# Weight sums of eight seven-product chunks: accumulating DMAs issued by GpSimd instead of VectorE additions

## The reference, cut to what matters

```
(sq, sk, sv, dq, dk, dv, iq, ik, iw, hq, hf, hi, hg,
 g_sb, g_dsa, g_hg) = jnp.split(h @ w_in_l, _split_points(), axis=-1)
...
mixed = jax.nn.sigmoid(g_sb) * y_sb + jax.nn.sigmoid(g_dsa) * y_dsa + jax.nn.sigmoid(g_hg) * y_hg
return mixed @ w_out_l
```

## Time and profile before

| what | value |
|---|---|
| median of three runs | 1595.08 us |
| span of the profiled execution | 1592.4 us |
| what lies around the span (median less span) | 2.7 us |
| PE (TensorE matmul) busy in the span | 1458.7 us (92%) |
| DVE (VectorE) busy | 740.9 us (47%) |
| ACT (ScalarE) busy | 314.6 us (20%) |
| POOL (GpSimd) busy | 22.7 us (1%) |
| moved by DMA | 380.17 MB, mean 239 GB/s |

### The profile page before, as it was taken

One profiled execution on the slowest core, in us unless ns is written; L12 is line 12 of the kernel. 1 busy time (PEld: TensorE's weight loads), 2 busy tenths in 40 slices (PEclk: granted clock), 3 DMA queues, 4 the chain that ended last, 5 costly groups with the idle time before them and its releaser, 6 DMA issues.

```text
span 1592.4 us, 19689 instructions
## 1 busy us (share of the span) xinstructions
PE 1458.7 (92%) x8156; PEld 1004.4 (63%) x8156; DVE 740.9 (47%) x1465; ACT 314.6 (20%) x655; POOL 22.7 (1%) x41
## 2 busy tenths in 40 slices
PE   8999999999999999999999999999999576577578
PEld 5687889999545788898999446755554133133132
DVE  3646576766666646567666656544331000001001
ACT  2234431122001125430222001334410000000000
POOL 0000000000000000000000002100000000000000
PEclk9999999999999999999999999999999788788689
DMA  9547224454453633334444446655799999999998
GB/s 319 191 159 245 90 100 153 157 199 169 158 175 108 213 127 138 107 107 159 159 169 182 179 158 204 226 185 186 287 392 426 427 426 426 428 427 426 428 419 318
DMA packets 114921, 380.17 MB, mean 239 GB/s; under 512 B 10836, under 2 KB 23252, under 8 KB 104144
## 3 DMA queue, kind: packets, MB, share of 16 engines
q1 hardware_dynamic: 111952, 369.53, 60.6%
q0 software_dynamic: 2880, 9.36, 1.9%
HBM read 377.25 MB, written 5.73 MB: 241 GB/s over the span
## 4 chain that ended last, share of the span: by engine, by line
PE 79%; DMA 17%; DVE 2%; SPq 1%; ACT 1%; issue 1%; DVEq 0%; ACTq 0%
DMA ring<-in_w 17%; PE bank L1508 13%; PE bank L1561 12%; PE bank L1144 11%; PE bank L1151 8%; PE bank L1324 5%; PE bank L1712 4%; PE bank L1298 3%; PE bank L1250 3%; PE bank L1274 2%; PE bank L1610 2%; PE bank L1738 1%; PE bank L1481 1%; PE bank L1483 1%; PE bank L1200 1%; PE bank L1226 1%
## 5 line engine op out<-in xcount | busy, mean ns | idle before, releaser
L1144 PE MATMUL bank<-hT,ring 128*128 128x256 f32 x832 | 185.4, 381 | 0.0
L1144 PEld LDWEIGHTS bank<-hT,ring 128*128 128x128 f32 x832 | 156.0, 190 | 21.9 <-issue 1.0
L1712 PE MATMUL bank<-ring,region 128*32 128x512 f32 x208 | 116.4, 724 | 48.8 <-DMA region<-in_w 48.8
L1712 PE MATMUL bank<-region 128*32 128x512 f32 x512 | 116.6, 722 | 48.5 <-DMA ring<-in_w 48.5
L1561 PE MATMUL bank<-region 128*128 128x512 f32 x320 | 140.6, 592 | 0.0
L1561 PEld LDWEIGHTS bank<-region 128*128 128x128 f32 x320 | 60.5, 190 | 74.6 <-issue 74.6
L1508 PE MATMUL bank<-region 128*128 128x128 f32 x768 | 100.5, 275 | 0.0
L1508 PEld LDWEIGHTS bank<-region 128*128 128x128 f32 x768 | 93.0, 192 | 0.0
L1712 PEld LDWEIGHTS bank<-region 128*32 128x32 f32 x512 | 29.1, 130 | 94.0 <-issue 94.0
L1712 PEld LDWEIGHTS bank<-ring,region 128*32 128x32 f32 x208 | 25.8, 130 | 83.3 <-issue 83.3
L1151 PE MATMUL bank<-ring,hT 128*128 128x512 f32 x160 | 71.7, 596 | 0.0
(11 more groups left out here) (488 smaller groups left out, 2421.6 us busy)
## 6 DMA issues: line engine op xcount, KB each, us to landing
region<-in_w SPq DMA_DIRECT2D x43, 2048.0 KB, 38.6
ring<-in_w SPq DMA_DIRECT2D x30, 2048.0 KB, 37.7
ring<-in_w_in SPq DMA_DIRECT2D x26, 2048.0 KB, 8.2
ring<-in_w_up SPq DMA_DIRECT2D x16, 2048.0 KB, 8.3
ring<-in_w_down SPq DMA_DIRECT2D x32, 1024.0 KB, 6.3
own_slot<-in_w SPq DMA_DIRECT2D x7, 2048.0 KB, 43.3
ring<-in_w_out SPq DMA_DIRECT2D x6, 2048.0 KB, 7.9
region<-in_w SPq DMA_DIRECT2D x22, 512.0 KB, 9.3
```

The costliest lines, as they stand in the source:

```text
L1144: t = mm(b[:, 0:T], w[:, k, :], act[:, k, :], start=(k == 0), stop=(k == KD - 1))
L1712: t = mm(b[32 * e:32 * e + 32, :], xg[:, k, 32 * e:32 * e + 32], four[e][c][:, 512 * (k % 2):512 * (k % 2) + 512], start=(k == 0), stop=(k ...
```

## The change

In eight of the ten chunks (all but `iq` and `hh` of layer 0) VectorE's four sums are taken out and GpSimd issues seven DMAs of 512 KB. Three are plain loads from the weights in DRAM: s1 gets a21, s2 gets a11, s4 gets a12. Four add into their destination: s1 += a22 (from DRAM), s2 += s1, s3 += a11 (from DRAM, onto a21 in the ring slot, so after the chunk has arrived), s4 += s2. The last three additions of the chain s1, s2, s4 each wait for the one before. An addition is all that such a DMA does here, so the signs of the scheme change: s2 = s1 + a11, s3 = a11 + a21, s4 = a12 + s2, with the signs carried by the activations' sums and the reassembly. `rooms` are the events after which the places of s1 and of s2 and s4 are free.

```
+ADDED = (("hf", 0), (4, 0), (5, 0), ("iq", 1), ("hh", 1), ("hf", 1), (4, 1), (5, 1))
...
-    s += [("gt",), ("gw", 4), ("ho",)]
+    s += [("gt",), ("ho",)]
...
-    s += [("gw", 5), ("gc", 4, 0)] + att[22:] + gm(4, 1, *GATE_ORDER) + [("gc", 4, 1), ("gs",), ("gf", 4, 0), ("gf", 4, 1)]
+    s += [("gc", 4, 0)] + att[22:] + gm(4, 1, *GATE_ORDER) + [("gc", 4, 1), ("gs",), ("gf", 4, 0), ("gf", 4, 1)]
...
+            def added_sums(l, c, rooms, parts):
+                (a11, a12), (a21, a22) = dram_quarters(l, c)
+                s1, s2, s3, s4 = row_weight_sums(l, c) if c in ROW_SEVENS else gate_sums(l, c)
+                n = 16 * (ADDED.index((c, l)) + 1)
+                pool.wait_ge(*rooms[0])
+                pool.dma_start(s1, a21).then_inc(sum_begun[0], 16)
+                pool.wait_ge(*rooms[1])
+                pool.dma_start(s2, a11).then_inc(sum_begun[1], 16)
+                pool.dma_start(s4, a12).then_inc(sum_begun[2], 16)
+                pool.wait_ge(sum_begun[0], n)
+                pool.dma_start(s1, a22, accum_op=ALU.add).then_inc(sum_added[0], 16)
+                pool.wait_ge(sum_begun[1], n)
+                pool.wait_ge(sum_added[0], n)
+                pool.dma_start(s2, s1, accum_op=ALU.add).then_inc(sum_added[1], 16)
+                for part in parts:
+                    pool.wait_ge(*arrive[chunk_at[(l, part)]])
+                pool.dma_start(s3, a11, accum_op=ALU.add).then_inc(sum_added[2], 16)
+                pool.wait_ge(sum_begun[2], n)
+                pool.wait_ge(sum_added[1], n)
+                pool.dma_start(s4, s2, accum_op=ALU.add).then_inc(sum_added[3], 16)
+            def forget_sums(l):
+                added_sums(l, "hf", [bk.full((l, "ty1", "iq"))] * 2, ["hf"])
+            def late_gate_sums(l):
+                added_sums(l, 4, [bk.full((l, "gy", "hf", 1))] * 2, [("g", 4)])
+                added_sums(l, 5, [bk.full((l, "ty1", "hh")), bk.full((l, "hl", LAST, 1))], [("g", 5)])
             rows, cols = 15, 31
+            forget_sums(0)
             pool.wait_ge(seg_normed, 1)
...
             pool.wait_ge(kv_stored, 16)
+            late_gate_sums(0)
+            added_sums(1, "iq", [bk.full((0, "ty1", "wo", 0))] * 2, ["iq"])
+            added_sums(1, "hh", [bk.full((0, "ty1", "wo", 1)), bk.full((0, "down", PRODUCTS[-1]))], ["hi", "hg"])
+            forget_sums(1)
+            late_gate_sums(1)
...
-                        pe.wait_ge(quarter_sums_ready, 12 * l + 4 * SEVENS.index(c) + GATE_ORDER.index(m) - 1)
+                        pe.wait_ge(*sum_there(l, c, GATE_ORDER.index(m) - 2))
...
-                link(V.tensor_tensor(r2, b22, r1, ALU.subtract))
+                link(V.scalar_tensor_tensor(out=r2, in0=b22, scalar=-1.0, in1=r1, op0=ALU.mult, op1=ALU.subtract))
...
-                V.tensor_tensor(pairs[:, 0:2, 1, :], eight[:, :, 1, :], bc(m5.unsqueeze(1), [2, P]), ALU.add)
+                V.tensor_tensor(gate_corners[t2][:, 1, :], gate_corners[t2][:, 1, :], m5, ALU.add)
+                V.scalar_tensor_tensor(out=gate_corners[t2][:, 3, :], in0=gate_corners[t2][:, 5, :], scalar=-1.0, in1=m5,
+                                       op0=ALU.mult, op1=ALU.subtract)
```

More of the change, by code:

```diff
@@ L545, in build @@
              "sums_ready neg_rs_ready up_sums_ready h_sums_ready m1_copied last_half_loaded row_quarter_sums raw_row_sums row_m1_copied rows_copied row_corners_used wo_quarter_sums wo_row_sums wo_m1_copied wo_added p_quarter_sums p_row_sums p_m1_copied p_rows_copied "
-             "quarter_sums_ready row_sums_ready seven_m1_copied seven_sigmoids").split()]
+             "row_sums_ready seven_m1_copied seven_sigmoids").split()]
         gate_row = [sem(f"gate_row{j}") for j in range(2)]
+        sum_begun = [sem(f"sum{j}_begun") for j in (1, 2, 4)]
+        sum_added = [sem(f"sum{j}_added") for j in (1, 2, 3, 4)]
         chunks = chunks_of_layer(0) + chunks_of_layer(1) + chunks_of_block2()
@@ L848, in gate_sums, with dram_quarters, sum_there @@
             return own_[:, 3], low_quarters[:, 0], a21, low_quarters[:, 1]
+        def dram_quarters(l, c):
+            w = a["w_in"][l].rearrange("(h k p) n -> h p k n", h=2, p=P)
+            first = {"iq": COL["iq"], "hh": COL["hi"], "hf": COL["hf"]}.get(c, COL["gsb"] + 512 * c if isinstance(c, int) else 0)
+            return [[w[kh][:, :, first + 256 * fh:first + 256 * fh + 256] for kh in range(2)] for fh in range(2)]
+        def sum_there(l, c, j):
+            return sum_added[j], 16 * (ADDED.index((c, l)) + 1)
         def row_weights(l, c):
@@ L1242, in row_products @@
                         pe.wait_ge(raw_row_sums, l + 1)
-                    if 2 <= n < 6:
-                        pe.wait_ge(row_quarter_sums, 8 * l + 4 * ROW_SEVENS.index(c) + n - 1)
+                    if 2 <= n < 6 and l:
+                        pe.wait_ge(*sum_there(l, c, n - 2))
+                    elif 2 <= n < 6:
+                        pe.wait_ge(row_quarter_sums, 4 * ROW_SEVENS.index(c) + n - 1)
                     if m in ROW_STARTS:
@@ L2322, in quarter_sums_of_rows @@
                 s1, s2, s3, s4 = row_weight_sums(l, c)
-                n = 8 * l + 4 * ROW_SEVENS.index(c)
+                n = 4 * ROW_SEVENS.index(c)
                 V.tensor_tensor(s1, a21, a22, ALU.add).then_inc(row_quarter_sums, 1)
                 dve.wait_ge(row_quarter_sums, n + 1)
-                V.tensor_tensor(s2, s1, a11, ALU.subtract).then_inc(row_quarter_sums, 1)
-                V.tensor_tensor(s3, a11, a21, ALU.subtract).then_inc(row_quarter_sums, 1)
+                V.tensor_tensor(s2, s1, a11, ALU.add).then_inc(row_quarter_sums, 1)
+                V.tensor_tensor(s3, a11, a21, ALU.add).then_inc(row_quarter_sums, 1)
                 dve.wait_ge(row_quarter_sums, n + 2)
-                V.tensor_tensor(s4, a12, s2, ALU.subtract).then_inc(row_quarter_sums, 1)
+                V.tensor_tensor(s4, a12, s2, ALU.add).then_inc(row_quarter_sums, 1)
             def raw_sums(l):
@@ L2351, in row_corner_sums @@
                 m5 = psum[bk.bank((l, "ty0", c))][:, 256:512]
-                free(V.tensor_tensor(pairs[:, 0:2, 1, :], eight[:, :, 1, :], bc(m5.unsqueeze(1), [2, 256]), ALU.add),
-                     (l, "ty0", c))
-                free(V.tensor_tensor(row_corners[:, 2, :], row_corners[:, 5, :], read((l, "ty1", c))[:, 0:256], ALU.subtract),
+                V.tensor_tensor(row_corners[:, 1, :], row_corners[:, 1, :], m5, ALU.add)
+                free(V.scalar_tensor_tensor(out=row_corners[:, 3, :], in0=row_corners[:, 5, :], scalar=-1.0, in1=m5,
+                                            op0=ALU.mult, op1=ALU.subtract), (l, "ty0", c))
+                free(V.tensor_tensor(row_corners[:, 2, :], read((l, "ty1", c))[:, 0:256], row_corners[:, 5, :], ALU.subtract),
                      (l, "ty1", c))
@@ L2476, in gate_row_sums @@
                 r1, r2, r3, r4 = [gate_rows_sums[late][:, j] for j in range(4)]
-                link(V.tensor_tensor(r1, b12, b11, ALU.subtract))
-                link(V.tensor_tensor(r2, b22, r1, ALU.subtract))
+                link(V.tensor_tensor(r1, b11, b12, ALU.subtract))
+                link(V.scalar_tensor_tensor(out=r2, in0=b22, scalar=-1.0, in1=r1, op0=ALU.mult, op1=ALU.subtract))
                 V.tensor_tensor(r3, b22, b12, ALU.subtract)
-                V.tensor_tensor(r4, r2, b21, ALU.subtract).then_inc(row_sums_ready, 1)
+                V.tensor_tensor(r4, r2, b21, ALU.add).then_inc(row_sums_ready, 1)
             def gate_corner_sums(l, c, t2):
```

29 lines of the change are left out of this document (6 added, 23 removed).

## The result

The changed kernel takes 1621.17 us (median of four runs, 1619.21 to 1624.42) against 1594.98 us for the kernel before on the same chip (four runs): 26.2 us slower, a ratio of 1.0167 with a 95% interval of 1.0156 to 1.0179. The prediction was 1595.1 us with a range up to 1612. It is wrong, and its direction is that of the rival *the chain of additions ends late*, which had a chance of 0.24.

What follows compares the result with a forecast made beforehand. TensorE was taken to bound the mixers, up to about 1150 us, and the streaming of expert weights the rest. Zero from VectorE's relief plus zero from new waits left 1595.1 us, no change; range 1593.5 to 1612.

Steps and rivals of the forecast that it cites:

- the chain of additions ends late: Rival: `hf` of layer 1 and chunk 5 in both layers end late, slower from 6.7 us per addition; chance 0.24.
- VectorE's relief: VectorE ends some 34 us less busy, worth nothing on the path because TensorE waits for none of it.
- zero: Gain in the mixers from VectorE's 34 us: none, with 3.2 us of listed waits the most that could come.
- the listed waits: TensorE's waits in the two mixers, 1.8 and 1.4 us, together 3.2, which removing VectorE's sums would not shorten.
- the sum of the chain: Loads, queue and three additions: 27.6 us in 29.05 at layer 1's `hf`, 22.2 in 25.86 at chunk 5.
- my upper bound, the copy done twice: Price limit of one adding DMA: the dearer plain transfer of 512 KB twice in a row, 14.2 us.
- Room enough: DMA engines, busy 0.54 around `hh` and `hf`, can take 28 MB more, 123 us spread over 600 us.
- Its formula: Late-chain rival's waits at `hf` of layer 1 and chunk 5 twice: 8 us per addition gives 1610, 10 gives 1628.
- the other case: The forecast of no change, 1595.1 us: every chain ends before the product that reads it; chance 0.65.
- the threshold of 6.7: Average us per addition up to which no change holds; there `hf` waits 2.5 and chunk 5 twice 0.3.
- The stopped issuer: Rival: GpSimd cannot hand out transfers while VectorE runs; layer 1's `hf` is 13.6 us late, 1609; chance 0.04.
- Issuing: GpSimd's handing out of the 56 DMAs at 0.56 us each, 32 us; chunk 5's three issues 1.7 us.

Runs made afterwards that it cites:

- e6_no_sums: Changed kernel with the eight chunks' sums made by nobody and no wait of TensorE for them: 1594.02 us, ratio 1.0000 to the kernel before.
- Experiment 3: Changed kernel with the four adding DMAs of each chunk made plain copies, same order and waits: 1595.26 us, ratio 1.0009 to the kernel before.
- e9_load_held: e5_more_room with SyncE's 2 MB load of layer 1's `hf` chunk held until the addition into s1 has landed: 1604.45 us, ratio 1.0062.
- e12_br_held: Changed kernel with SyncE's 2 MB of branch weights held until chunk 5's addition into s1 has landed, both layers: 1622.60 us, ratio 1.0180.
- e5_more_room: Changed kernel with DMA_SCRATCH, taken as the room for GpSimd's descriptors, at 2816 in place of 2048: 1604.67 us, ratio 1.0066.
- e10_some_room: Changed kernel with DMA_SCRATCH at 2304 in place of 2048: 1603.48 us, ratio 1.0057.
- e4_s1_early: Changed kernel with chunk 5's addition into s1 issued before GpSimd waits for the places of s2 and s4: 1607.73 us, ratio 1.0082.
- e1_dve_three: Changed kernel with the sums of layer 1's `hf` and both layers' chunk 5 back on VectorE: 1594.26 us, ratio 1.0000 to the kernel before.
- e8_seven_early: Changed kernel with only layer 1's `hf` back on VectorE and chunk 5's addition into s1 issued early: 1594.56 us, ratio 1.0002.
- e11_seven_room: Changed kernel with only layer 1's `hf` back on VectorE and DMA_SCRATCH at 2816: 1593.77 us, ratio 0.9996.

## Why the prediction was wrong

**What bounds the kernel, and VectorE's relief: right.** The sum's "zero" for the 34 us taken from VectorE is what e6_no_sums measures, and the listed waits that I said would stay (L1390, L1424, L1439 of before) stand unchanged.

**The step that failed** is the sum of the chain: "Cost: 7.1 + 4.4 + 7.1 + 4.5 + 4.5 = 27.6. It fits by 1.4 us", and with it 22.2 for chunk 5. Its parts against GpSimd's timeline, each from one issue to the next and the last to the product that reads s4:

| part of the chain, us | assumed | `hf`, layer 1 | chunk 5, layer 0 | chunk 5, layer 1 |
|---|---|---|---|---|
| up to the issue of the addition into s1 | 11.5 / 6.1 | 8.4 | 4.5 | 4.5 |
| addition into s1 | 7.1 | 11.7 | 11.9 | 12.0 |
| addition into s2 | 4.5 | 8.7 | 5.3 | 5.9 |
| addition into s4 | 4.5 | 7.8 | 10.1 | 9.5 |
| sum | 27.6 / 22.2 | 36.6 | 31.8 | 31.9 |
| there was room for | 29.05 / 25.86 | | | |

The loads were cheaper than I took them, the additions 1.7 times as dear: 9.1 to 9.4 us each on average in place of 5.4, where the forecast held up to 6.7. Three things were missing from the price that I took from the nearest rows.

- *The work of an addition.* I put an SBUF addition at 4.5 by counting passes over the bytes. Experiment 3 shows 336 packets for 144 and about twice the time on the engines. In work, my upper bound, the copy done twice, was the better picture.
- *The neighbours.* "Room enough" rested on a DMA share of 0.54 over 50 us. Over the chain of `hf` itself, from 534 to 571, the changed kernel has 1.09, which means full. The additions wait for each other, so what counts is how full the engines are while one is in flight, and each release that starts a chain also starts a 2 MB load of SyncE (`hf`) or stands just before one (chunk 5). An addition into s1 with little beside it, chunk 4 of layer 0, went from issue to the next in 6.6 us (167.11 to 173.68) at a DMA share of 0.53. e9_load_held brings `hf`'s from 13.1 to 7.2 us by taking the load away, and e12_br_held chunk 5's, from issue to landing, from 11.3 to 6.9.
- *The room for descriptors.* It was in no step and in no rival. In chunk 5 it delays the first addition by 3 us, which puts two additions behind 2 MB each; with more room (e5_more_room, e10_some_room) TensorE waits for neither chunk 5. It is one of two sufficient cures: with 2048 as before, taking one addition out of the chain does it as well (e4_s1_early). At `hf` more room takes 2 to 4 us off the 10.9 by single profiles; the rest is gone only where `hf` of layer 1 has no adding DMAs (e1_dve_three, e3_plain, e8_seven_early, e11_seven_room).

The figure of the Trainium skill that the prediction set beside this, page "DMA: Bandwidth & Descriptors", section "Anatomy of one DMA — SWDGE (gpsimd) path", is an estimate of 3.2 us for a plain transfer of 512 KB. The trace does not agree at these places: the plain loads into s1 land after 6.3 to 11.8 us. In e3_plain the fastest copies inside SBUF land after 2.9.

**The rival: right in place and direction.** It named the three chains that became late and no other. Its formula at 9.3 us per addition gives 1595.1 + 10.4 + 2 x 8.1 = 1621.7, close to the 1621.2 measured, but by luck, because two errors cancel: it has the loads 1.6 to 3.1 us too dear at each place, and it lacks the slow products behind the waits (6.3 us together). The forecast stayed with the other case because the threshold of 6.7 lay above the chosen prices by less than their error; between bounds of 3.0 and 14.2 us that margin was no ground for a chance of 0.65. The range ended at 1612, a little over 8 us per addition, for the same reason.

**The stopped issuer: not seen.** `iq`'s last product releases `hf`'s places at 534.16, by SyncE's load, and GpSimd's first load follows at 534.55, while DVE is busy for 5.9 of the 9 us up to 543. **Issuing** was underpriced too, with little effect: 0.75 to 1.6 us in place of 0.56, so that chunk 5's three issues take 2.8 us in place of 1.7.

## What to carry to other kernels

Price a transfer in a chain by rows from a stretch as full as the one in which it will run, at the moment of its release, not by the mean DMA share around it: the addition into s1 took 6.6 us with little beside it and 12 to 13 beside a 2 MB load. Where a chain of dependent steps fits into its window by 5% and the price of a step is known only within a factor of nearly five, do not count on its fitting. Look for a chain's head start (issuing the addition whose input is already there) or leave the three tight chunks to the engine that has time for them. Work taken off an engine for which nobody waits is worth nothing: a kernel that simply leaves the work out measures that directly.

## What the runs showed of the hardware

- An accumulating DMA of 512 KB is 336 packets against 144 for a plain one and holds the 16 DMA engines for about 3.2 us against 1.5 (an estimate from the queue's shares). GpSimd hands it out in 0.9 us (inside SBUF; 1.4 to 1.7 directly behind another addition) or 1.3 to 1.6 us (from DRAM), against 0.55 and 0.75.
- The room for GpSimd's descriptors acts as a threshold. At 2048 an accumulating DMA behind two plain ones of 512 KB is handed out 3 us late, at 2304 and 2816 at once; the whole kernel is 16 to 18 us faster for it. The Trainium skill, page "DMA: Bandwidth & Descriptors", section "SWDGE vs HWDGE vs iDMA", says that GpSimd appends descriptors to rings in SBUF; the late issue and its cure agree with rings that are full, and no row shows the rings themselves.
- A wait of TensorE of 4 to 5 us costs more than itself: the granted clock fell to 0.57 behind it (the lower of the two levels, 1.2 GHz, would be 0.50), groups of eight matmuls took up to 2.08 us in place of 1.06, and 1.5 to 3 us more were lost at each place.
